# A two-layer decoder step with experts: gather without gaps, shared down products later, gather batches of four passes

## Chip, cores and metric

The kernel runs on 1 core of a Trainium2 chip. The metric is the device time of one execution in microseconds, median of the runs.

## What is computed

One inference step of a two-layer decoder for 320 tokens (256 of a prompt, 64 of 8 sampled sequences), model width 1024: layer 0 mixes with sliding-window attention, layer 1 with gated linear attention. Each is followed by the mixture of experts that this study is about:

```python
def moe(h, router_w, router_b, wg, wu, wd, swg, swu, swd):
...
    scores = jax.nn.sigmoid((x @ router_w).astype(jnp.float32))
    sel = scores + router_b.astype(jnp.float32)
...
    _, eidx = lax.top_k(jnp.where(emask, sel, -jnp.inf), TOP_K)
    w = jnp.take_along_axis(scores, eidx, axis=1)
    w = w / jnp.sum(w, axis=-1, keepdims=True) * ROUTED_SCALE
    routed = routed_experts(x, eidx, w.astype(x.dtype), wg, wu, wd)
    shared = (jax.nn.silu(x @ swg) * (x @ swu)) @ swd
    return (routed + shared).reshape(B, S, D)
```

`emask` leaves the best 4 of 8 groups of experts, so each token goes to 8 of 64 experts. An expert has gate and up weights of 1024 x 256 each (2 MB together in float32) and down weights of 256 x 1024 (1 MB). All 64 experts of both layers are read once: 3 MB x 64 x 2.

## The kernel before

Everything is in one `decoder_step`. `moe(l)` first routes: it counts the tokens of each expert, ranks the experts by their counts (ranks 0 and 1 are fixed experts whose weights are loaded ahead), and writes the ranking to `order`. Then 28 passes follow, with 128 slots each. A pass holds two or three experts by rank: `pass_plan` gives (96, 32), (64, 64) or, at the places `LIGHT_AT`, (64, 32, 32) slots. `posS` holds for each token and expert the slot of the token in the expert's list, and `excess` whether any expert has more tokens than its slots; then `rest` goes through all 64 experts once more.

What one pass does on TensorE (PE), in `moe`, from L2026 on:

- *gate product* (L2044): the pass's tokens from the buffer `xg`, in groups of 32 or 64 columns, times the gate and up weights of its experts, 8 steps over the model width, into bank `W0`.
- *fills* (L1946): part of the gather for the next batch of passes. The gather is a product of the token rows (`htok`, `htok2`, high and low parts, five matmuls) with a selection matrix `sel` (a one where slot and token meet). A batch is 2 or 4 passes (`BATCHES`), so 256 or 512 columns; a batch needs 8 fills, one per 128 rows of the model width (batch 0: 4 fills with two rows blocks each). ScalarE (ACT) and VectorE (DVE) copy the fills in turns from banks `W1` and `W2` to `xg` (L2110, L2169), in which each fill overwrites tokens already used.
- *turning* (L2070): `hh`, which DVE made from `W0` (silu by ACT at L2127, product and weight by DVE at L2209), is transposed; ACT copies it to `hTs`. In a batch's last pass the slot weights of the next batch are made too (`slot_weights`, L1956), from the selection in bfloat16, `selb`, which DVE makes in `dense`.
- *combine* (L1974, L1976): the last pass's result (`yhi`, `ylo`) is added to the tokens' sums, by a product with `gt`, 12 matmuls.
- *down product* (L2094), into `W1` and `W2`. ACT and DVE then take them to `yhi` and `ylo`.
- in passes 1 and 2 the shared expert's down products, `shared_down` (L2022), which add to the same sums.

DVE makes the selections of the batch after the next (`select`, L2149 and L2154, then `dense`, L2163) at the end of a batch's last pass.

The weights are moved by one queue, issued by SyncE (SP) in `expert_stream`. Gate and up weights go to `gu_ring`, 6 places of 2 MB; down weights to `dn_ring`, 5 places of 1 MB. Ahead of the wait for `order` come the down and gate/up weights of ranks 0 and 1 and the shared expert's down weights (L1605, 1 MB, in the fifth place). Behind it `load_up` (L1614) and `load_down` (L1622) alternate in the order of the passes. A place is free again when the pass that used it has made its gate product (`gu_full`) or its down product (`y_full`), the fifth place when `shd_used` tells that the shared products are made. SyncE issues strictly in order, so a load that waits for a place holds all behind it. `DN_EARLY` = 4 down loads need no free place.

## Time and profile before

| | us |
|---|---|
| median of 3 runs | 1434.81 (1434.44 to 1436.46) |
| profiled execution | 1434.92 |
| its span, first to last instruction | 1433.1 |
| PE busy | 1395.9 (97%) |
| DVE busy | 437.7 (31%) |
| ACT busy | 317.1 (22%) |
| queue of SyncE | 489.96 MB, 82.1% of the span of 16 engines |

The span is 1.8 us shorter than the time of the same execution. The passes of layer 0 take from 247.5 to some 706 us, those of layer 1 from 954.5 to 1412. PE's busy time is no rate: a matmul that is in the array counts as busy. A window's GB/s tells how full the transfers' side is.

### The profile page before, as it was taken

Reading aid. Unit: us, or ns where it says so; the run is one execution under the profiler, and the core shown is the slowest. Engines: PE = TensorE matmul, PEld = TensorE weight load, DVE = VectorE, ACT = ScalarE, POOL = GpSimd, SP = SyncE. Lnnn points to the kernel's source line nnn. Section 1 sums busy time; section 2 is a strip of 40 time slices with the busy share of each in tenths; the row PEclk is TensorE's granted clock in tenths of the full one; section 3 lists DMA queues with packets and bytes.
Section 4 is the critical chain, followed back from the end, with each engine's and each line's share of the span. In section 5 each row is a group of like instructions: output and inputs, shape, how many; then the busy total and the mean of one; then the engine's idle time right before and its main releaser. Section 6 shows DMA issues by size and latency. Waiting matters only on the chain.

```text
span 1433.1 us, 20787 instructions
## 1 busy us (share of the span) xinstructions
PE 1395.9 (97%) x8288; PEld 706.4 (49%) x8288; DVE 437.7 (31%) x1161; ACT 317.1 (22%) x746; POOL 48.1 (3%) x86
## 2 busy tenths in 40 slices
PE   7999999999999999999999999999999999999997
PEld 3345657444445444444465456564444444444443
DVE  1146535312221222122345243442121312122214
ACT  2134323111111111111345113411111111111113
POOL 0100302000000000000100010010000000000000
PEclk9999999999999999999999999999999999999998
DMA  9999528999999999999972245389999999999993
GB/s 393 389 381 427 214 103 311 392 390 427 421 423 426 421 425 425 424 426 424 422 320 118 118 162 219 112 336 380 425 424 423 426 423 421 425 424 426 425 424 126
DMA packets 48002, 509.52 MB, mean 356 GB/s; under 512 B 5808, under 2 KB 6208, under 8 KB 8320
## 3 DMA queue, kind: packets, MB, share of 16 engines
q1 hardware_dynamic: 44144, 489.96, 82.1%
q0 software_dynamic: 3760, 18.20, 3.4%
q8 instruction: 68, 1.11, 0.3%
q14 instruction: 30, 0.25, 0.0%
HBM read 499.10 MB, written 11.01 MB: 356 GB/s over the span
## 4 chain that ended last, share of the span: by engine, by line
PE 88%; DMA 4%; DVE 3%; ACT 3%; issue 1%; SPq 0%; DVEq 0%; ACTq 0%
PE bank L2044 26%; PE banks L2094 13%; PE banks L1946 10%; PE banks L442 5%; PE ybank L1974 3%; PE banks L1119 3%; PE banks L1974 3%; PE bank L1976 3%; DMA s_gu_ring<-in_moe_up_dram 3%; PE bank L504 2%; PE ybank L1738 1%; PE banks L1738 1%; DMA s_gu_ring<-in_ada_w_dram 1%; PE banks L697 1%; PE banks L1124 1%; PE banks L671 1%
## 5 line engine op out<-in xcount | busy, mean ns | idle before, releaser
L2044 PE MATMUL bank<-s_gu_ring,s_hbuf 128*32 128x512 f32 (+1 forms) x2688 | 395.2, 593 | 1.4 <-DVE s_hbuf L2169 0.9
L2044 PEld LDWEIGHTS bank<-s_gu_ring,s_hbuf 128*32 128x32 f32 (+1 forms) x2688 | 121.9, 119 | 265.9 <-issue 265.9
L2094 PE MATMUL banks<-s_dn_ring,s_hTs 128*32 128x512 f32 (+1 forms) x1344 | 204.2, 596 | 0.0
L2214 DVE TENSOR_TENSOR s_ylo<-banks,s_yhi 128x512 fp32r<-128x512 f32 x112 | 77.5, 692 | 320.2 <-ACT s_yhi L2136 320.2
L1946 PE MATMUL banks<-s_sel,s_htok 128*128 128x512 f32 (+1 forms) x640 | 144.8, 374 | 0.5 <-issue 0.5
L1946 PEld LDWEIGHTS banks<-s_sel,s_htok 128*128 128x128 f32 x640 | 106.2, 188 | 60.7 <-issue 44.3
L2136 ACT CAST s_yhi<-banks 128x512 fp32r<-128x512 f32 x112 | 65.7, 586 | 296.5 <-PE banks L2094 296.5
L2209 DVE SCALAR_TENSOR_TENSOR s_hh<-s_sg,s_wsl,bank 128x256 f32<-128x256 f32 x56 | 26.9, 480 | 288.1 <-ACT s_sg L2127 288.1
L2094 PEld LDWEIGHTS banks<-s_dn_ring,s_hTs 128*32 128x32 f32 (+1 forms) x1344 | 55.9, 118 | 118.0 <-issue 117.3
L2127 ACT ACTIVATE s_sg<-bank 128x256 f32<-128x256 f32 x56 | 21.6, 385 | 364.8 <-PE bank L2044 364.8
L2169 DVE COPY s_hbuf<-banks 128x512 f32<-128x512 f32 (+1 forms) x60 | 39.4, 656 | 96.0 <-PE banks L1946 96.0
L1119 PE MATMUL banks<-s_gu_ring,s_hbuf 128*128 128x512 f32 x128 | 55.9, 593 | 0.5 <-DVE s_rs L1439 0.5
L2110 ACT COPY s_hbuf<-banks 128x512 f32<-128x512 f32 (+1 forms) x60 | 33.5, 559 | 57.9 <-PE banks L1946 57.9
L1974 PE MATMUL ybank<-s_yhi,s_gt 128*128 128x512 f32 x108 | 38.7, 439 | 0.0
L1119 PEld LDWEIGHTS banks<-s_gu_ring,s_hbuf 128*128 128x128 f32 x128 | 24.2, 191 | 29.1 <-issue 28.2
L504 PE MATMUL bank<-s_gu_ring,s_condT 128*32 128x512 f32 x288 | 34.9, 598 | 1.2 <-DMA s_gu_ring<-in_ada_w_dram 1.2
L2131 ACT COPY s_hTs<-bank 128x256 f32<-128x256 f32 x56 | 20.9, 373 | 64.0 <-PE bank L2070 43.1
L442 PE MATMUL banks<-s_hbuf,s_gu_ring 128*128 128x320 f32 x128 | 34.9, 433 | 0.0
L442 PE MATMUL banks<-s_qk,s_gu_ring 128*128 128x320 f32 x128 | 34.9, 433 | 0.0
L1974 PE MATMUL ybank<-s_ylo,s_gt 128*128 128x512 f32 x108 | 33.9, 395 | 0.0
L1974 PE MATMUL banks<-s_yhi,s_gt 128*128 128x512 f32 x108 | 33.9, 395 | 0.0
L1974 PE MATMUL banks<-s_ylo,s_gt 128*128 128x512 f32 x108 | 33.6, 392 | 0.0
(463 smaller groups left out, 1452.5 us busy)
## 6 DMA issues: line engine op xcount, KB each, us to landing
s_gu_ring<-in_moe_up_dram SPq DMA_DIRECT2D x128, 2048.0 KB, 15.2
s_dn_ring<-in_moe_wd_dram SPq DMA_DIRECT2D x128, 1024.0 KB, 12.8
s_gu_ring<-in_ada_w_dram SPq DMA_DIRECT2D x24, 2048.0 KB, 13.0
s_gu_ring<-in_win_dram SPq DMA_DIRECT2D x6, 2048.0 KB, 12.8
s_gu_ring<-in_wqkv_dram SPq DMA_DIRECT2D x6, 1024.0 KB, 19.4
s_gu_ring<-in_wo_dram SPq DMA_DIRECT2D x2, 2048.0 KB, 18.8
s_gu_ring<-in_shared_up_dram SPq DMA_DIRECT2D x2, 2048.0 KB, 9.8
s_gu_ring<-in_gwo_dram SPq DMA_DIRECT2D x2, 2048.0 KB, 10.8
```

The source lines that it names most:

```text
L442: last = pe.matmul(b[:, 0:T], item(slot)[:, k, (m % 4) * P:(m % 4 + 1) * P], src[:, k, :], start=(k == 0), stop=(k == KC - 1))
L504: last = pe.matmul(ada_bank(n)[32 * j:32 * j + 32, :], condT[:, k, lo:lo + 32], item(s)[:, k, :], start=(x == 0 and kk == 0), stop=(ends_g ...
L1119: last = pe.matmul(b[:, :], hT[:, k, t0:t0 + P], w[:, k, :], start=(k == 0), stop=(k == KC - 1))
L1946: last = pe.matmul(b[:, width * x:width * x + width], w[:, m * P:(m + 1) * P], sel[:, s, 0:width], start=(n == 0), stop=(n == 4))
L1974: last = pe.matmul(acc[(t, half)], g[:, t * P:(t + 1) * P], y[:, half, :], start=(p == 0 and y is yhi), stop=False)
L1976: last = pe.matmul(bank[6][:, :], g[:, 320 - 64 * half:448 - 64 * half], y[:, half, :], start=(p == 0 and y is yhi and half == 0), stop=False)
L2044: last = pe.matmul(W0[o:o + n, :], tokens_of(p, k)[:, o:o + n], w[:, k, :, :], start=(k == 0), stop=(k == KC - 1))
L2094: last = pe.matmul((W1, W2)[half][o:o + n, :], hTs[:, f, o:o + n], dn_ring[:, DN_PLACE[dn_of[(l, r)][0]], w0:w0 + 512], start=(f == 0), st ...
L2110: act.copy(fill_target(q, f), fill_source(q, f)).then_inc(S["fill_act"], 1)
L2136: act.copy(yhi[:, half, :], (W1, W2)[half]).then_inc(S["y_high"], 1)
L2169: dve.tensor_copy(fill_target(q, f), fill_source(q, f)).then_inc(S["fill_dve"], 1)
L2214: dve.tensor_tensor(ylo[:, half, :], (W1, W2)[half], yhi[:, half, :].bitcast(F32), ALU.subtract).then_inc(S["y_low"], 1)
```

## The change

Four things are changed, all in the expert part of both layers.

1. *Packed gather.* `ROOMS` gives a room to each rank of each layer, at most its slots, and `PITCH` a width to each batch: 112 columns a pass in batch 0, 104 in the others. `sel` has only the rooms, side by side, so fills are 448 or 416 columns wide. The gate product still has groups of 32 or 64 columns; it reads them from the packed place (`back_by`). The bfloat16 selection keeps 128 slots a pass: `spread` (in place of `dense`) zeroes it and copies each expert's columns to their slots. The gap columns of `xg` are zeroed once per layer. `excess` is now against the rooms.
2. *Batches.* Seven of four passes. Batch 0 has 8 fills of four passes ahead of pass 0, and passes 0 and 1 carry two fills each in place of four. Passes 24 to 27 carry none.
3. *Shared expert.* Its down weights are loaded within the stream, in a place of `dn_ring` that becomes free behind pass 16 in layer 0, and its down products are in passes 18 and 19. `DN_EARLY` is 5.
4. The pairs of experts in a pass are put together in another order; the numbers of experts and slots of each pass stay. `sg` and `hTs` now lie in the free space of `router`, and `selb` is one tile.

```diff
-NGU, NDN, DN_EARLY = 6, 5, 4
+NGU, NDN, DN_EARLY = 6, 5, 5
...
+PITCH = (112, 104, 104, 104, 104, 104, 104)
...
+def gathered(l, experts):
+
+    out, at = [], 0
+    for r, cap, o in places(experts):
+        out.append((r, ROOMS[l][r], o, at))
+        at += ROOMS[l][r]
+    return out
...
-BATCHES = (2, 4, 4, 4, 4, 4, 4, 2)
+SHD_PASS = 18
+BATCHES = (4,) * 7
...
-NFILL = 4 + 8 * (NB - 1)
+NFILL = 8 * NB
...
-            freed = [None] * (NDN - 1) + [2]
+            freed = [None] * NDN
+            shd_at = sum(len(experts) for experts in PASSES[l][:SHD_PASS + 1])
...
+                if i == shd_at:
+                    d = i % NDN
+                    down_in[d].n += 16
+                    shd_of.append((d, down_in[d].n, last_dn[d]))
+                    last_dn[d], freed[d] = (S["shd_used"], l + 1), SHD_PASS + 1
+                d = (i + (i >= shd_at)) % NDN
+                used = None if i < NDN else last_dn[d]
...
-                sp.dma_start(dn_ring[:, DN_PLACE[NDN - 1], :], a["shared_down"][l]).then_inc(down_in[NDN - 1].h, 16)
...
+                    if shd_of[l][2] == (S["y_full"], 2 * (l * NP + p + 1)):
+                        d, _, used = shd_of[l]
+                        sp.wait_ge(*used)
+                        sp.dma_start(dn_ring[:, DN_PLACE[d], :], a["shared_down"][l]).then_inc(down_in[d].h, 16)
...
-                        width = P * BATCHES[q]
...
+                        width = PITCH[q] * BATCHES[q]
+                        for n, (w, s) in enumerate(shown):
+                            last = pe.matmul(b[:, 0:width], w[:, f * P:(f + 1) * P], sel[:, s, 0:width], start=(n == 0), stop=(n == 4))
...
-                    for f in range(4):
+                    for f in range(8):
...
-                        fill_some(turns[:3])
-                        if p == 2:
+                        fill_some(turns)
+                        if p == SHD_PASS + 1:
...
-                        fill_some(turns[3:])
...
-                        if p == 1:
-                            pe.wait_ge(down_in[NDN - 1].h, shd_n)
+                        if p == SHD_PASS:
+                            pe.wait_ge(down_in[shd_d].h, shd_n)
...
+                    def spread(q):
+
+                        step(dve.memset(selb[:, :, 0:P * BATCHES[q]], 0.0))
+                        w = PITCH[q]
+                        for h in range(BATCHES[q]):
+                            for r, n, o, at in gathered(l, PASSES[l][BATCH_START[q] + h]):
+                                last = dve.tensor_copy(selb[:, :, h * P + o:h * P + o + n], sel[:, :, h * w + at:h * w + at + n].bitcast(F32))
                         return last
...
+                    dve.wait_ge(S["fill_full"], filled(0, 1))
+                    dve.memset(hbuf[:, :].rearrange("p (x s) -> p x s", s=P)[:, :, PITCH[0]:P], 0.0)
+                    for f in range(1, 8, 2):
+                        fill_out(0, f)
```

How the order of instructions moves. On SyncE, ahead of the first load of layer 0 that needs the order (`s_order` is the ranking, `ISA` reads it into a register), before:

```order
L1598 DMA s_dn_ring<-in_moe_wd_dram 128x2048 x2
L1602 DMA s_gu_ring<-in_moe_up_dram 128x4096 x2
L1605 DMA s_dn_ring<-in_shared_down_dram 128x2048
L1610 TENSOR_LOAD s_order
L1610 ISA x2
```

And in the changed kernel the shared expert's load, which stands behind the three gate/up loads that pass 16 of layer 0 lets go:

```order
L1633 ISA x2
L1637 ISA
L1637 DMA s_gu_ring<-in_moe_up_dram 128x4096
L1660 DMA s_dn_ring<-in_shared_down_dram 128x2048
L1641 TENSOR_LOAD s_order
```

The 1 MB load has moved from ahead of the stream of expert loads into it, where down loads stand behind it.

On PE, from the last fill ahead of pass 0 of layer 0 through pass 0 (gate product, fills, turning, down product), before:

```order
L1946 MATMUL banks<-s_sel,s_htok_0 128x256
...
L1956 MATMUL bank<-s_wpartS,s_selb 128x18
L2044 MATMUL bank<-s_gu_ring,s_hbuf 64x512 x16
L1946 MATMUL banks<-s_sel,s_htok 128x512 x4
L1946 MATMUL banks<-s_sel,s_htok_0 128x512
...
L2070 MATMUL bank<-s_cst,s_hh 128x128 x2
...
L2094 MATMUL banks<-s_dn_ring,s_hTs 64x512 x8
```

And now:

```order
L1964 MATMUL banks<-s_sel,s_htok_0 128x448
L1973 MATMUL bank<-s_wpartS,s_selb 128x12 x3
L1973 MATMUL bank<-s_wpartS,s_selb 128x18 x6
...
L2061 MATMUL bank<-s_gu_ring,s_hbuf 64x512 x16
L1964 MATMUL banks<-s_sel,s_htok 128x416 x4
...
L2087 MATMUL bank<-s_cst,s_hh 128x128 x2
L2110 MATMUL banks<-s_dn_ring,s_router 64x512 x8
```

Each fill is a row of four and a row of one; pass 0 had four such pairs of 512 columns, three ahead of the turning and one behind, and has two of 416.

On DVE, ahead of the copies that empty the first fills of layer 0, before:

```order
L2149 TENSOR_TENSOR s_sel<-s_cst,s_posS 128x3x128
...
L2178 TENSOR_TENSOR s_wpartS<-s_hh,s_wpartS 128x3x64
L2163 CAST s_router<-s_sel 128x256 x2
L2163 CAST s_selb<-s_sel 64x256
L2182 TENSOR_TENSOR s_ovh<-s_ovh,ybank 128x320
L2169 COPY s_hbuf<-banks 128x2x256 x2
```

And now:

```order
L2163 TENSOR_TENSOR s_sel<-s_cst,s_posS 128x3x60
...
L2189 TENSOR_TENSOR s_wpartS<-s_hh,s_wpartS 128x3x64
L2170 MEMSET s_selb 128x768
L2174 CAST s_selb<-s_sel 128x3x60
L2174 CAST s_selb<-s_sel 128x3x52
...
L2193 TENSOR_TENSOR s_ovh<-s_ovh,ybank 128x320
L2196 MEMSET s_hbuf 128x32x16
L2180 COPY s_hbuf<-banks 128x4x112 x4
```

Four selections have become ten, three casts a zeroing and ten casts (of which two are shown), and the gap columns are zeroed ahead of the copies.

## Rows read from the trace of the kernel before

**Rows 1.** The page, sections 1 and 2 (DMA: busy tenths in 40 slices).

```profile
PE 1395.9 (97%) x8288; PEld 706.4 (49%) x8288; DVE 437.7 (31%) x1161; ACT 317.1 (22%) x746; POOL 48.1 (3%) x86
...
DMA  9999528999999999999972245389999999999993
```

**Rows 2.** Windows: us, busy per engine (instructions), PEclk, DMA share, GB/s.

```profile
237.00:310.00 73.00, 72.31 (x442) 36.99 (x445) 24.17 (x69) 10.73 (x23) 0.00 (x0) 1.00 0.95 394
310.00:692.00 382.00, 381.65 (x2396) 178.19 (x2392) 87.98 (x214) 59.58 (x125) 0.00 (x0) 1.00 1.01 424
943.00:1010.00 67.00, 66.30 (x394) 35.36 (x394) 22.21 (x62) 9.70 (x21) 0.00 (x0) 1.00 0.95 389
1010.00:1398.00 388.00, 388.00 (x2254) 181.92 (x2253) 89.23 (x216) 60.27 (x126) 0.00 (x0) 1.00 1.01 424
```

**Rows 3.** Chain of waits at the end of layer 0 (start us, us, what).

```profile
670.33 21.34 DMA s_gu_ring<-in_moe_up_dram
```

**Rows 4.** Timeline of PE, passes 26 and 27 of layer 0.

```profile
687.81 3.64 PE L2094 MATMUL banks<-s_dn_ring,s_hTs 128*32 128x512 f32 x32
691.80 7.07 PE L2044 MATMUL bank<-s_gu_ring,s_hbuf 128*32 128x512 f32 x64 [0.35 <-DMA s_gu_ring<-in_moe_up_dram]
```

**Rows 5.** Three gate/up loads of layer 0, by tile and window.

```profile
L1614 SPq DMA_DIRECT2D s_gu_ring<-in_moe_up_dram x1: 338/338/338, 241.6 to 241.6; - x1
...
DMA to landing us min/median/max: 15.2/15.2/15.2
...
L1614 SPq DMA_DIRECT2D s_gu_ring<-in_moe_up_dram x1: 347/347/347, 254.8 to 254.8; - x1
...
DMA to landing us min/median/max: 7.7/7.7/7.7
...
L1614 SPq DMA_DIRECT2D s_gu_ring<-in_moe_up_dram x1: 338/338/338, 270.5 to 270.5; - x1
...
DMA to landing us min/median/max: 9.3/9.3/9.3
```

**Rows 6.** Chain of waits, layer 0, first fills to pass 4.

```profile
241.58 5.04 PE banks L1946 x40
...
270.25 3.63 PE banks L1946 x15
...
282.76 3.63 PE ybank L2022 x8
286.39 7.00 PE bank L2044 x64
...
295.91 3.43 PE banks L2022 x8
299.34 1.87 PE bank L2022 x8
...
307.98 6.87 PE bank L2044 x64
...
323.91 6.42 PE bank L2044 x57
```

**Rows 7.** Timeline of DVE ahead of pass 0, layer 0.

```profile
241.83 0.49 DVE L2182 TENSOR_TENSOR s_ovh<-s_ovh,ybank 128x320 f32<-128x320 f32 x1 [1.17 <-ACT s_ovh L1814]
...
248.32 2.31 DVE L2154 TENSOR_TENSOR s_sel<-s_cst,s_posS 128x192 fp32r<-128x192 f32 x9
```

**Rows 8.** Groups of instructions by form, DVE, the casts of L2163.

```profile
L2163 DVE CAST s_router<-s_sel 128x512 bf16<-128x512 f32 x24 | 9.2, 423 | 0.4
...
L2163 DVE CAST s_router<-s_sel 128x256 bf16<-128x256 f32 x8 | 2.0, 288 | 0.1
```

**Rows 9.** Line L360 on PE (ns min/median/max, first to last start).

```profile
L360 PE MATMUL banks<-s_sq,s_cst x32: 432/445/457, 194.5 to 720.7; 128*32 128x320 f32 x32
...
L360 PE MATMUL ybank<-s_sq,s_cst x16: 433/741/742, 8.2 to 12.6; 128*32 128x320 f32 x16
```

**Rows 10.** Windows, the end of the span.

```profile
1430.00:1433.00 3.00, 0.00 (x0) 0.00 (x0) 0.00 (x0) 0.00 (x0) 0.00 (x0) 0.50 0.74 243
```

More of the change, by code:

```diff
@@ L1927, in fills_in @@
                         return []
-                    return range(4 * j, 4 * j + 4) if q == 0 else range(2 * j, 2 * j + 2)
+                    return range(2 * j, 2 * j + 2)
                 def last_of(p):
@@ L2199, in _ @@
                     step(select(1))
-                    dense(1).then_inc(S["sel_full"], 1)
+                    spread(1).then_inc(S["sel_full"], 1)
                     dve.wait_ge(S["wall_full"], l * NB + 1)
```

108 lines of the change are left out of this document (41 added, 67 removed), and 6 rows, old and new, of the table ROOMS.

## The prediction

> **What bounds the kernel now.** I read the page first: TensorE is busy for 97% of the span, and in the long stretches of expert work the DMA line stands at 9 as well [rows 1]. Two resources are full at once, so the share of busy time does not say which of them sets the end. The windows are read next. From 310 to 692 us the transfers run at 424 GB/s without a dip, and so do those of layer 1 from 1010 to 1398; in the stretches ahead of these (237 to 310, 943 to 1010) the means are only 394 and 389 GB/s [rows 2]. The lost time there is 73 x (1 - 394/424) = 5.2 us and 67 x (1 - 389/424) = 5.5 us. Third, the chain at the end of layer 0: the last pass starts when the gate/up weights of its last expert land; the chain goes back through this transfer for 21.34 us [rows 3]. That transfer was issued 21 us before it landed, so it did not wait for a free place, it waited for the transfers in front of it. The matmuls were nearly as late: pass 26's down products end at 687.81 + 3.64 = 691.45, and the wait from there is 0.35 us [rows 4]. So both resources reach the last pass together, and the transfers are the later one. From here on, time comes off only if **the stream of weight transfers ends earlier**.
>
> What ends the stream: it begins when the sorted order is known, moves fixed bytes at 424 GB/s, and loses time only where the queue runs empty because a place in the ring is not free yet. The sixth gate/up load is issued at 241.6 and lands 15.2 us later, at 256.8. The next needs the place of pass 0's expert, is issued at 254.8, and lands 7.7 us after it, at 262.5 [rows 5]. One such load takes 2,097,152 B / 424 GB/s = 4.9 us when the queue is full; so a load that finds the queue empty starts 2.8 us after its issue, and 262.5 - 256.8 - 4.9 = 0.8 us is lost here. The two other losses of layer 0 follow the long passes 1 and 2: pass 2 starts at 286.39 and pass 3 at 307.98 [rows 6], 21.6 us apart, where a pass of the steady loop takes 15.9 us (307.98 to 323.91). In passes 1 and 2 PE also runs the shared expert's down products, in pass 1 double fills too.
>
> **The change, part by part.**
>
> *Shared down weights.* Their 1 MB is loaded today before the order is known, when the queue has nothing else. Now it sits inside the stream: 1,048,576 B / 424 GB/s = **+2.5 us per layer**. The fifth early down load moves 1 MB ahead of the first empty queue; it adds no bytes, but prefetch now lasts until 256.8 + 2.5 = 259.3.
>
> *Shared down products.* They cost 3.63 + 3.43 + 1.87 = 8.9 us on PE [rows 6]. They leave passes 1 and 2 and come back in 18 and 19: nothing for PE's sum, but the places of passes 1 and 2 come free earlier.
>
> *Packed gather.* 15 fill matmuls of 512 columns take 3.63 us, 0.242 each, and 40 of 256 columns 5.04 us, 0.126 each [rows 6]: 0.45 ns a column. At 416 columns a fill matmul costs 0.199, at 448 0.213. A steady pass has 10: -0.43 us. PE per layer: passes 0 and 1 lose 20 matmuls of 512 (-4.8) and 2 x 0.43; passes 2 to 21 20 x 0.43 = -8.6; passes 22 and 23 widen from 256 to 416 (+1.5); passes 24 and 25 have none (20 x 0.126 = -2.5). Sum -15.3 us. All of it lies beside the transfers, so I cost it at nothing; its cover is the stream, and what PE gains turns into waits for weights.
>
> *The first batch.* Pass 0 cannot start before all 8 fills of four passes: 40 x 0.213 = 8.5 us in place of 5.0, +3.5; six more small weight matmuls, +0.5. VectorE now makes ten selections (1,344 elements) in place of four (768), zeroes the spread copy, copies ten pieces, then zeroes the gap columns of the token buffer before it may empty the second bank. Selections cost 1.05 ns an element and 0.08 us each, by nine with 1,536 elements in 2.31 us [rows 7]: +1.0 us. The zeroing isn't in the trace: 768 words at between nothing and that rate, up to 0.8; the copies, 1.4 to 2.2 by the rates of a cast (288 ns for 256 elements, 423 for 512: 0.53 ns an element [rows 8]) and of a selection. The chain today ends with the product at 241.83 + 0.49 = 242.3 [rows 7]; the new one at about 243.5 to 244.8, then gap columns 0.2 to 0.6 and the copy out 0.6. The fourth fill should start at 241.6 + 3 x 1.07 = 244.8, and would then start at up to 246.1. So pass 0 starts **4.1 us later** (no delay by VectorE) **to 5.4**; I take 5.0, nearer to the high end since every piece of that chain is a small instruction.
>
> The Trainium skill says in "VectorE: DVE Perf Modes" (What auto-detection actually checks) that a copy with one source may double its rate when source and destination are in SBUF and their outermost dimensions agree, which these copies meet; the 0.53 ns a cast pays today agrees. By the page alone the copies take the lower 1.4 us and pass 0 starts some 0.5 us earlier.
>
> *Effect on the empty queue.* Issue of the first load that needs a freed place: 254.8 + 5.0 = 259.8, start 262.6, queue empty since 259.3: **3.3 us** lost, 2.4 to 3.7 by the bounds. Pass 0 has two fills where it had four and shrinks to about 13.5 us (7.0 gate product, 2.0 fills, 0.9 turning, 3.6 down product), so pass 1 starts at 266.0 and frees its three places at 273.1, while the down loads before run until 277.4. Today the load issued at 270.5, just behind two down loads, lands 9.3 us after its issue, 1.6 us more than the lone one [rows 5], so a narrow margin does not help fully. With 4 us I take a loss of 0.3, and 0 to 1 as bounds. Later passes are 15.5 us and issue well ahead. So 3.6 us per layer replace 5.2 and 5.5.
>
> **Sum.** Layer 0: -5.2 + 3.6 + 2.5 = +0.9; layer 1: -5.5 + 3.6 + 2.5 = +0.6. Together +1.5 us on the profiled execution's 1434.92, and the median of the runs is 0.1 lower: **1436.3 us**. With all bounds: 2 x (2.4 + 2.5) - 10.7 = -0.9, and 2 x (4.7 + 2.5) - 10.7 = +3.7. PE is ready for the last pass 15.3 - 5.0 = some 10 us before its weights, less what it waits earlier (the down weights of passes 2 and 18, which stand behind gate/up loads or the shared MB in the queue). SyncE's added issue costs nothing, since transfers there wait some 10 us in the queue.
>
> **Rivals.** *The clock falls in the new waits (slower).* PE now idles for some 4 us ahead of pass 27 of both layers. No idle stretch of that length lies between the passes today. At the start, where PE comes out of idleness, the 128x320 matmuls from 8.2 to 12.6 us show a median of 741 ns against 445 later [rows 9], so some 4 us ran slow; and in the span's last 3 us, with PE done, the granted clock is 0.50, the 1.2 GHz level [rows 10]. If pass 27 restarts so, half of that is lost, 2 us per layer and 4 in all: 1440.3. It decides from a wait of that order on; for it speaks that waits gather at the end of the layer, against it that passes 2, 16 and 18 may take most of the 10 us, where lost clock only shortens the later wait. The Trainium skill, "TensorE: Matmul & The Clock Gate" (HAM oscillation), has this rule: waiting for a DMA between bursts of matmuls sends the clock to 1.2 GHz, and the next burst starts cold. By it I give this 15%.
>
> *The early losses vanish (faster).* If pass 0 starts no more than 1.7 us later and nothing is lost behind pass 1, the whole 10.7 us is saved and 5.0 paid: 1429.1. Half of it gives 1432. The four-pass first batch speaks against it; for it speaks that pass 2 alone starts 5 us earlier than today even so. 17% for over 0.2%.
>
> *VectorE becomes late at each batch.* After a batch's last pass it selects (2.0 us), zeroes (to 0.8) and spreads (1.4 to 2.0), starting 1.8 us into a gate product of 7.0 us: done at 6.0 to 6.9, in time. If it overran by 2.5 us, six times a layer, 15 us would exceed PE's 10 us of slack: +5 per layer, 1446. 9%.
>
> *The rooms are too small.* Then the loop over 64 experts runs: 64 x 3 MB at 424 GB/s is 475 us. Working through the routing of the reference's inputs gives no expert above its room: 1%.
>
> **How the numbers follow.** No change beyond 0.2% (2.9 us, about what a measurement can tell) is the likeliest, 58% for this case with 1433.9 to 1438.6 as its own range, of which 5 in 58 lie over the bound. Faster 17; same 53; slower 5 + 15 + 9 + 1 = 30. The range leaves one in ten on each side: 1431.5 to 1440.5.
>
> **What would show it.** Right: 424 GB/s from about 280 us on in layer 0, one dip near 260, none near 293; pass 0 about 5 us later, pass 3 about 10 us earlier (near 297); waits of PE for weight transfers of some 8 to 10 us per layer, where now there is 0.4; last pass still released by its gate/up transfer, within 1.5 us of 691.8. Wrong: a last pass that starts right behind pass 26, a dip at 293 that stays, or a granted clock below 1.00 behind the waits.

## The result and the profile after

| | before | after |
|---|---|---|
| median, us | 1435.16 (12 runs, 1434.44 to 1436.67) | 1438.35 (12 runs, 1437.21 to 1441.09) |
| ratio, with its 95% interval | | 1.002 [1.0012, 1.0028] |
| profiled execution, us | 1434.92 | 1437.59 |
| its span, us | 1433.1 | 1435.8 |
| PE busy, us | 1395.9 | 1379.5 |

The change costs 3.2 us, 0.22%, just over the 0.2% that can be told from nothing. TensorE's busy time shrank by 16.4 us and the end came later. The chain that ended last, section 4 of the page of the kernel before:

```profile
PE 88%; DMA 4%; DVE 3%; ACT 3%; issue 1%; SPq 0%; DVEq 0%; ACTq 0%
```

And the page of the kernel after, its sections 1, 2, 4 and 5 (to be held against [rows 1]):

```profile
PE 1379.5 (96%) x8208; PEld 705.5 (49%) x8208; DVE 445.2 (31%) x1281; ACT 312.2 (22%) x740; POOL 48.0 (3%) x86
...
DMA  9999526999999999999972245279999999999992
...
PE 77%; DMA 14%; DVE 4%; ACT 3%; issue 1%; SPq 1%; DVEq 0%; ACTq 0%
...
L2061 PE MATMUL bank<-s_gu_ring,s_hbuf 128*32 128x512 f32 (+1 forms) x2688 | 397.1, 596 | 8.1 <-DMA s_gu_ring<-in_moe_up_dram 7.1
...
L2110 PE MATMUL banks<-s_dn_ring,s_router 128*32 128x512 f32 (+1 forms) x1344 | 207.6, 602 | 12.3 <-DMA s_dn_ring<-in_moe_wd_dram 11.4
```

The last numbers of the two lower rows are TensorE's waits ahead of the gate products (L2061) and the down products (L2110): 18.5 us for weight transfers, over both layers. In the chain the transfers' share rose from 4 to 14%. The span grew by 2.7 us while the busy time fell by 16.4, so TensorE stood idle for 19.1 us more, nearly all of it in these waits. The windows of the kernel after (us, busy per engine, granted clock, DMA share, GB/s), beside [rows 2]:

```profile
237.00:310.00 73.00, 69.35 (x460) 37.61 (x461) 25.13 (x81) 11.77 (x26) 0.00 (x0) 1.00 0.97 408
310.00:692.00 382.00, 375.07 (x2328) 176.63 (x2326) 91.82 (x264) 56.32 (x119) 0.00 (x0) 1.00 1.01 425
553.30:556.50 3.20, 3.20 (x10) 1.20 (x8) 0.00 (x0) 0.12 (x1) 0.00 (x0) 0.50 1.01 430
692.00:699.00 7.00, 6.76 (x48) 2.37 (x52) 0.00 (x0) 0.00 (x0) 0.00 (x0) 0.76 1.04 433
940.00:1010.00 70.00, 66.05 (x421) 36.45 (x423) 24.94 (x83) 11.80 (x25) 3.99 (x2) 1.00 0.96 403
1010.00:1400.00 390.00, 384.51 (x2214) 183.38 (x2206) 92.89 (x266) 57.72 (x123) 0.00 (x0) 1.00 1.01 425
```

Two things are to be seen. The early dip is shallower than before, but still there: 73 x (1 - 408/425) = 2.9 us in layer 0 and 70 x (1 - 403/425) = 3.6 us in layer 1, where it was 5.2 and 5.5. And the granted clock is no longer 1.00 all through the layers: it is 0.50, the 1.2 GHz level, in a window of pass 18 of layer 0 (and in one of pass 18 of layer 1, from 1263.2 us), and on the mean 0.76 in the seven microseconds around the start of pass 27 of layer 0. The timeline of PE in the kernel after, at four places (start us, us, line, then in brackets the wait ahead of it). They are the start of the count, pass 18 of layer 0, and pass 27 of both layers:

```profile
224.38 0.20 PE L1782 MATMUL bank<-s_mb,s_upper_b 128*128 128x64 bf16 x1 [0.61 <-ACT s_htok L1831]
...
552.92 5.35 PE L2110 MATMUL banks<-s_dn_ring,s_router 128*64 128x512 f32 x16 [3.40 <-DMA s_dn_ring<-in_moe_wd_dram]
...
692.24 8.77 PE L2061 MATMUL bank<-s_gu_ring,s_hbuf 128*32 128x512 f32 x64 [3.32 <-DMA s_gu_ring<-in_moe_up_dram]
...
1401.32 7.07 PE L2061 MATMUL bank<-s_gu_ring,s_hbuf 128*32 128x512 f32 x64 [3.21 <-DMA s_gu_ring<-in_moe_up_dram]
```

The third and fourth rows are the same product, pass 27's, in layer 0 and layer 1. Behind a wait of 3.32 us it takes 8.77 us, behind one of 3.21 us 7.07, the value that it had before [rows 4]. The difference, 1.70 us, is the fall of the clock: it stands at 0.50 from 693.2 to 696.6 us, and half of these 3.4 us is lost. Pass 18's product shows the same: 5.35 us, where it takes 3.65 in run noload1, whose clock didn't fall there.

The first row gives a mark: L1782 is the first product of the count of the tokens, with which the expert part of a layer begins. With it and the start of pass 27, an execution falls into pieces that can be compared between kernels. A is from the count to pass 27 of layer 0, B from there to the count of layer 1, C from there to pass 27 of layer 1, D from there to the end. All from the timelines of PE, in us:

| kernel | A | B | C | D | span |
|---|---|---|---|---|---|
| before | 467.5 | 239.5 | 467.4 | 34.4 | 1433.1 |
| after | 467.9 | 241.2 | 467.9 | 34.5 | 1435.8 |

In these two kernels pass 27 starts when its weights land, so A and C show the transfers' side; B and D show what the clock costs behind that. Of the 2.7 us that the span grew by, 0.35 are in A, 0.53 in C, and **1.7 in B**. B is the 1.70 us of pass 27's gate product.

The first load that waits for a freed place, in the kernel after (queue and landing, as in [rows 5]):

```profile
L1637 SPq DMA_DIRECT2D s_gu_ring<-in_moe_up_dram x1: 341/341/341, 259.4 to 259.4; - x1
...
DMA to landing us min/median/max: 7.9/7.9/7.9
```

The transfer ahead of it landed at 259.7, it landed at 267.3; a full queue takes 4.9 us for it, so 2.7 us are lost. The same reading behind pass 1 (issued at 272.9, landed 5.8 us behind the one ahead of it) gives 0.9. The third loss, behind pass 2, is not seen any more: that pass's freed places are filled behind a full queue (a load issued at 275.1 lands 17.7 us later).

### The profile page after: what moved, and what is told of

Its sections match the earlier page's. It is cut to its first block, busy times and chain, and to the rows that moved or that the text cites. A ratio compares the mean times of both kernels' runs of the same rounds, so it can differ in the third digit from the quotient of the medians.

```text
span 1435.8 us, 20741 instructions
## 1 busy us (share of the span) xinstructions
PE 1379.5 (96%) x8208; PEld 705.5 (49%) x8208; DVE 445.2 (31%) x1281; ACT 312.2 (22%) x740; POOL 48.0 (3%) x86
## 4 chain that ended last, share of the span: by engine, by line
PE 77%; DMA 14%; DVE 4%; ACT 3%; issue 1%; SPq 1%; DVEq 0%; ACTq 0%
PE bank L2061 22%; PE banks L2110 12%; DMA s_gu_ring<-in_moe_up_dram 7%; PE banks L1964 6%; DMA s_dn_ring<-in_moe_wd_dram 6%; PE banks L459 5%; PE banks L1136 3%; PE ybank L1991 3%; PE banks L1991 3%; PE bank L1993 3%; PE bank L521 2%; PE banks L1764 1%; DMA s_gu_ring<-in_ada_w_dram 1%; PE banks L714 1%; PE banks L1141 1%
## 5 line engine op out<-in xcount | busy, mean ns | idle before, releaser
L2061 PE MATMUL bank<-s_gu_ring,s_hbuf 128*32 128x512 f32 (+1 forms) x2688 | 397.1, 596 | 8.1 <-DMA s_gu_ring<-in_moe_up_dram 7.1
L2061 PEld LDWEIGHTS bank<-s_gu_ring,s_hbuf 128*32 128x32 f32 (+1 forms) x2688 | 124.1, 119 | 272.3 <-issue 272.3
L2110 PE MATMUL banks<-s_dn_ring,s_router 128*32 128x512 f32 (+1 forms) x1344 | 207.6, 602 | 12.3 <-DMA s_dn_ring<-in_moe_wd_dram 11.4
L1964 PEld LDWEIGHTS banks<-s_sel,s_htok 128*128 128x128 f32 x560 | 100.5, 188 | 44.7 <-issue 42.5
L2110 PEld LDWEIGHTS banks<-s_dn_ring,s_router 128*32 128x32 f32 (+1 forms) x1344 | 57.7, 119 | 131.7 <-issue 130.4
L1964 PE MATMUL banks<-s_sel,s_htok 128*128 128x416 f32 (+1 forms) x560 | 120.9, 363 | 1.2 <-DVE s_hbuf L2180 0.7
L2222 DVE SCALAR_TENSOR_TENSOR s_hh<-s_router,s_wsl,bank 128x256 f32<-128x256 f32 x56 | 26.9, 480 | 287.7 <-ACT s_router L2143 287.7
L2143 ACT ACTIVATE s_router<-bank 128x256 f32<-128x256 f32 x56 | 21.5, 385 | 373.4 <-PE bank L2061 373.4
L2180 DVE COPY s_hbuf<-banks 128x416 f32<-128x416 f32 (+1 forms) x56 | 33.3, 594 | 64.8 <-PE banks L1964 64.8
L2126 ACT COPY s_hbuf<-banks 128x416 f32<-128x416 f32 (+1 forms) x56 | 28.6, 510 | 47.8 <-PE banks L1964 47.8
L2147 ACT COPY s_router<-bank 128x256 f32<-128x256 f32 x56 | 20.9, 374 | 66.4 <-PE bank L2087 35.5
## 6 DMA issues: line engine op xcount, KB each, us to landing
s_gu_ring<-in_moe_up_dram SPq DMA_DIRECT2D x128, 2048.0 KB, 21.5
s_gu_ring<-in_wo_dram SPq DMA_DIRECT2D x2, 2048.0 KB, 19.1
```

The source lines that it names most:

```text
L1964: last = pe.matmul(b[:, 0:width], w[:, f * P:(f + 1) * P], sel[:, s, 0:width], start=(n == 0), stop=(n == 4))
L2061: last = pe.matmul(W0[o:o + n, :], tokens_of(p, k)[:, o - back_by[r]:o - back_by[r] + n], w[:, k, :, :], start=(k == 0), stop=(k == KC - 1))
L2110: last = pe.matmul((W1, W2)[half][o:o + n, :], hTs[:, f, o:o + n], dn_ring[:, DN_PLACE[dn_of[(l, r)][0]], w0:w0 + 512], start=(f == 0), st ...
L2126: act.copy(fill_target(q, f), fill_source(q, f)).then_inc(S["fill_act"], 1)
L2180: dve.tensor_copy(fill_target(q, f), fill_source(q, f)).then_inc(S["fill_dve"], 1)
```

## The experiments

Theory: the end of A and C is set by the stream of transfers, with three terms (the time that the queue runs empty at the start, the shared expert's megabyte in the stream, the moment at which pass 0 frees its place); B and D pay for falls of the clock behind waits ahead of the last passes. Rivals: TensorE or VectorE, late since pass 0, carries that to the end; or the clock is without effect. The eleven runs take the change apart along its parts ("packed" takes in the new order of the pairs, part 4, which no run separates from the packing). In run noload only layer 0 can be read; the other ten are in the table, with the pieces of their profiled executions. Four kernels (late, b24pre, pre, preawake) have 1.5 to 1.7 us in B from a fall of the clock between the layers, near 877 us, in a stage that no run changed; the last section comes back to it.

| kernel | packed | shared late | batches | A | B | C | D | span |
|---|---|---|---|---|---|---|---|---|
| before | no | no | of 2, 4 | 467.5 | 239.5 | 467.4 | 34.4 | 1433.1 |
| late | no | yes | of 2, 4 | 467.0 | 241.2 | 467.1 | 34.4 | 1433.8 |
| b24pre | yes | no | of 2, 4 | 467.9 | 242.6 | 466.9 | 36.1 | 1438.2 |
| b24 | yes | yes | of 2, 4 | 464.9 | 241.2 | 464.2 | 37.3 | 1432.2 |
| pre | yes | no | of 4 | 467.7 | 243.7 | 468.1 | 36.0 | 1439.7 |
| after | yes | yes | of 4 | 467.9 | 241.2 | 467.9 | 34.5 | 1435.8 |
| awake | as after | | | 467.9 | 239.5 | 468.0 | 34.4 | 1434.6 |
| preawake | as pre | | | 467.8 | 242.7 | 468.4 | 34.4 | 1437.5 |
| b24awake | as b24 | | | 466.2 | 239.5 | 464.2 | 34.4 | 1428.7 |
| best | as b24 | | | 464.2 | 239.5 | 464.1 | 34.4 | 1426.5 |
| b24wait | as b24 | | | 469.7 | 240.8 | 469.9 | 37.1 | 1441.7 |
| noload1 | as after | | | 467.8 | 240.9 | 465.2 | 36.1 | 1434.3 |

### awake: no bare wait ahead of pass 27

```diff
                         if l * NP + p:
                             pe.wait_ge(S["hT_full"], l * NP + p)
+                        if p == NP - 1:
+                            keep_awake(pe, W0, 14)
```

`keep_awake` is the kernel's own helper (L437): products of 128 columns into a bank that the gate product overwrites. Each of them stands in the trace as two matmuls.

> Theory (the stream of the experts' transfers sets the end, and the fall of the clock behind the 3.3 us wait ahead of pass 27 is paid on top): 14 products without a use in that wait keep the granted clock at 1.0, pass 27 and the combination behind it run at full speed, and 1.6 us come off in layer 0 and nothing in layer 1, whose wait of 3.18 us was followed by no fall in the profiled execution; 1436.7 us beside 1435.2 of the kernel before, ratio 1.001. If the fall comes in both layers in most executions, 3.2 us come off: 1435.1, ratio 1.000. Rival (the clock matters nowhere, since TensorE has time to spare): 1438.3, ratio 1.002.

Measured: 1435.68 us (11 runs) beside 1435.56, ratio 1.0002 [0.9993, 1.0011]; the change's own interval, [1.0012, 1.0028], lies wholly above it. The change's excess over before is gone: 0.1 us is left of 3.2. Timeline of PE ahead of pass 27 of layer 1, and the window of pass 27 in layer 0:

```profile
1396.86 3.39 PE L440 MATMUL bank<-s_cst 128*128 128x128 f32 x28
1400.18 7.07 PE L2063 MATMUL bank<-s_gu_ring,s_hbuf 128*32 128x512 f32 x64
```

```profile
692.00:699.00 7.00, 7.00 (x67) 2.88 (x69) 0.00 (x0) 0.00 (x0) 0.00 (x0) 1.00 1.04 428
```

The clock stays at 1.00 where it was 0.76. A and C are those of after within 0.13 us: the added products take nothing from the transfers' side; B is back at 239.5. The medians differ by 2.7 us (3.1 when each is held against the kernel before in its own session), where one fall costs 1.7, so some executions of the changed kernel seem to have more than one; the profiled one had one that costs. All twelve of them (from 1437.21 us) lie at least 1.9 us above the fastest of awake (1435.34). The fall of pass 18 (at 554.2 and 1260.8 in this trace) is still there and costs nothing at the end, since TensorE waits again before pass 27. The rival "the clock matters nowhere" is out.

### noload and noload1: the price of the megabyte

```diff
 # noload, in both layers; noload1 the same for l == 1 only
-                    down_in[d].n += 16
...
-                        sp.dma_start(dn_ring[:, DN_PLACE[d], :], a["shared_down"][l]).then_inc(down_in[d].h, 16)
```

> Leaves out the shared expert's load of 1 MB; its products are done with whatever lies in that place. Theory (stream): the last gate and up weights land 2.5 us sooner in each layer, 5.0 in all: 1433.3 us, ratio 0.9987; with the shorter wait ahead of pass 27 (0.8 us instead of 3.3) the clock doesn't fall there either, and 1.6 more come off: 1431.7, ratio 0.9976. Rival (TensorE or VectorE, late by the 5 us of the late start, carries that to the end): 1438, ratio 1.002, and no idle time ahead of pass 27 changes.

Measured: 4275.49 us. The time as a whole says nothing: with layer 0's result changed, layer 1 routes otherwise, and the loop over all 64 experts, which is entered when a room is too small, runs from 1440 to 4243 us. Only layer 0, which is not touched by that, can be read: from the count (224.03) to pass 27 (689.45) it takes 465.4 us where the change takes 467.9. That is 2.45 us for 1 MB. To have the same within a whole execution, the load was left out in layer 1 only:

> The change without the shared expert's load of layer 1 (whose products are done with whatever lies in that place); layer 0 is left whole, so that the routing of layer 1 is that of the reference. Theory (stream, a megabyte at 424 GB/s): the last weights of layer 1 land 2.5 us sooner, 466.0 us behind the start of its stage in place of 468.5, and the wait ahead of pass 27 shrinks to 0.7 us: 1435.1 to 1435.8 us, ratio 1.000. Rival (TensorE ends near the stream): the last 1 us or so of it is not had, 1437, ratio 1.001.

Measured: C = 465.2 in place of 467.9, 2.7 us less, and A unchanged at 467.8. That is the stream's price of the megabyte, as the theory had it. But the time is 1438.4 us, ratio 1.0013 [1.0003, 1.0022], not 1.000. The timeline of PE at pass 27 of layer 1 says why:

```profile
1398.22 8.73 PE L2062 MATMUL bank<-s_gu_ring,s_hbuf 128*32 128x512 f32 x64 [4.87 <-DMA s_gu_ring<-in_moe_up_dram]
```

My expectation of a shorter wait was wrong. Here is the down product of pass 18 of layer 1, in the change first, then in noload1:

```profile
1262.07 5.35 PE L2110 MATMUL banks<-s_dn_ring,s_router 128*64 128x512 f32 x16 [3.44 <-DMA s_dn_ring<-in_moe_wd_dram]
1258.98 3.65 PE L2111 MATMUL banks<-s_dn_ring,s_router 128*64 128x512 f32 x16 [0.98 <-DMA s_dn_ring<-in_moe_wd_dram]
```

Without the load TensorE waits 2.46 us less there, and the clock doesn't fall, which saves another 1.70. So it comes to pass 27 some 4.2 us sooner, the weights only 2.7; it waits 4.87 us, not 3.21, the clock falls, and the product takes 8.73 us, not 7.07. A wait taken from one pass turned up in the last, where it costs. Layer 0 of this run, whose edit is that of the change, shows what a fall in pass 18 does for the last wait: in this execution the clock fell in pass 2 (behind a wait of 1.94 us) and not in pass 18, and the wait ahead of pass 27 is 4.96 us, where the change's, behind a fall in pass 18, is 3.32.

### late, b24pre, b24: which part of the change does what

`late` is the kernel before with the shared part alone (the lines of the diff above on `DN_EARLY`, `SHD_PASS`, `shd_at` and `shd_of`, and nothing else), `b24pre` the kernel before with the packed gather alone (and the new order of the pairs), `b24` both with the old batches. Against the changed kernel b24 is (in all kernels of this form the last expert's selection in a pass reaches to the pass's width, so that no column of `sel` is left unwritten):

```diff
-PITCH = (112, 104, 104, 104, 104, 104, 104)
+PITCH = (112, 112, 104, 104, 104, 104, 104, 104)
...
-BATCHES = (4,) * 7
+BATCHES = (2, 4, 4, 4, 4, 4, 4, 2)
...
-NFILL = 8 * NB
+NFILL = 4 + 8 * (NB - 1)
...
-                        fill_some(turns)
+                        fill_some(turns[:3])
...
+                        fill_some(turns[3:])
```

> The kernel before with the late shared load and products alone: batches and unpacked gather as before. Theory (two limits near each other): the stream has a place more full at its start and loses 3.8 us less there, against 2.5 us for the shared megabyte in it; but TensorE's work, which ended 0.35 us ahead of the last weights before, becomes the limit, and the late products still stand in it: the same as before or up to 1 us slower, 1435.2 to 1436.5, ratio 1.000 to 1.001. Rival (the stream alone bounds): 1.3 us less per layer, 1432.6, ratio 0.998. Rival (the megabyte costs its 2.5 us in full): 5 more, 1440, ratio 1.0035.

> The packed gather alone: shared load and products, and the batches, as in the kernel before. Theory (TensorE and the stream both end near 691 us of layer 0 in the kernel before, and with the packing the stream alone is left): the last weights land where the kernel before has them or up to 1.5 us sooner per layer, since nothing in the stream is changed but places that come free sooner; with waits of 3 to 4 us ahead of passes 26 and 27 the clock falls behind them, as in the run pre, which costs up to 2 us per layer: 1433 to 1438 us, likeliest 1436, ratio 1.000. Rival (TensorE's work bounds the kernel before, so the 15 us of it that the packing saves in each layer come off in part): 1425, ratio 0.993.

> The batches of the kernel before (2, 4, 4, 4, 4, 4, 4, 2) with the packed gather and the late shared products kept. Theory (stream): pass 0 starts some 4.7 us sooner, near 247.5, the first load that waits for a place is issued near 255 and no longer finds the queue empty (2.7 us of loss gone, at most 1 left behind pass 1): the last weights land 1.7 to 2.7 us sooner in each layer, 1433 to 1435 us, ratio 0.9985 to 1.0; the wait ahead of pass 27 gets no shorter, so the clock may fall as before. Rival (the batches are at no fault: the queue runs empty for another reason, as the time from a place coming free to the landing): same as the change, 1438, ratio 1.002.

Measured: late 1434.11 us, ratio 0.9988 [0.9979, 0.9998]; b24pre 1440.02 us, ratio 1.0027 [1.0016, 1.0038]; b24 1431.71 us, ratio 0.9967 [0.9955, 0.9979].

*late.* Its window of the early passes and its timeline at the end of layer 0:

```profile
237.00:310.00 73.00, 72.30 (x479) 38.80 (x478) 25.21 (x71) 11.96 (x26) 0.00 (x0) 1.00 1.01 426
```

```profile
687.69 3.64 PE L2104 MATMUL banks<-s_dn_ring,s_hTs 128*32 128x512 f32 x32
691.14 2.33 PE L2054 MATMUL bank<-s_gu_ring,s_hbuf 128*32 128x512 f32 x20
```

```profile
PE 91%; DVE 3%; ACT 3%; DMA 1%; issue 1%; SPq 0%; DVEq 0%; ACTq 0%
```

426 GB/s from the start, so the early loss of 5.2 us [rows 2] is gone in full. What is left of it in A is 0.5 us: pass 27 starts right behind pass 26 with no wait, and the chain (third fence) holds 1% of transfers, beside 4% before. TensorE is the limit, and it ends only 0.5 us ahead of where the transfers did. B is 1.7 us longer than before, though pass 27's product takes 7.05 us: this execution, the slowest of the ten, has the fall between the layers. I had expected no gain; 1.1 us came in the median. The rival by which the transfers alone bound the kernel before is out, and so is the one with the full 2.5 us per layer.

*b24pre.* Windows of the early passes and of pass 26 of layer 0, then the timeline of passes 26 and 27:

```profile
237.00:310.00 73.00, 72.06 (x454) 37.39 (x456) 26.49 (x88) 10.46 (x23) 0.00 (x0) 1.00 0.97 398
672.10:678.90 6.80, 6.00 (x32) 1.67 (x36) 0.00 (x0) 0.00 (x0) 0.00 (x0) 0.50 1.02 424
```

```profile
672.90 10.02 PE L2064 MATMUL bank<-s_gu_ring,s_hbuf 128*32 128x512 f32 x64 [2.90 <-DMA s_gu_ring<-in_moe_up_dram]
...
692.60 7.85 PE L2064 MATMUL bank<-s_gu_ring,s_hbuf 128*32 128x512 f32 x56 [2.91 <-DMA s_gu_ring<-in_moe_up_dram]
```

The early dip stays (398 GB/s beside 394), A and C move by +0.4 and -0.5, and TensorE, with less to do, waits ahead of passes 26 and 27, and the clock falls there. (The second row is cut by the end of its view: the whole product of 64 matmuls takes 8.71 us.) The packing alone makes the kernel 4.8 us slower, 2 us beyond the slow end of what I expected: it gives the stream nothing (I had reckoned with up to 1.5 us per layer), and pays 3.1 us in B, of which 1.6 are pass 27's product and 1.5 the fall between the layers, and 1.7 in D. The rival (it saves TensorE's time at the end) is out.

*b24.* Both together: window of the early passes and of the end of layer 1, pass 27 of layer 1 in the timeline, and the first load that waits for a place:

```profile
237.00:310.00 73.00, 72.07 (x492) 39.46 (x494) 27.56 (x90) 11.74 (x26) 0.00 (x0) 1.00 1.01 426
1393.90:1400.70 6.80, 5.84 (x28) 1.59 (x32) 0.00 (x0) 0.00 (x0) 0.00 (x0) 0.50 0.86 357
```

```profile
1394.86 9.96 PE L2071 MATMUL bank<-s_gu_ring,s_hbuf 128*32 128x512 f32 x64 [4.75 <-DMA s_gu_ring<-in_moe_up_dram]
```

```profile
L1637 SPq DMA_DIRECT2D s_gu_ring<-in_moe_up_dram x1: 341/341/341, 255.1 to 255.1; - x1
...
DMA to landing us min/median/max: 9.8/9.8/9.8
```

Issued 4.3 us sooner than in the changed kernel, that load lands 9.8 us later, behind a full queue: nothing is lost, and A and C are 2.6 and 3.1 us below those before. By the terms: 5.2 and 5.5 us of early losses gone, 2.5 of the megabyte added, -2.7 and -3.0. That is more than I expected of the run, since no loss at all is left behind pass 1 either. The late shared part frees the stream, but TensorE is then the limit and hides it; the packing frees TensorE, but the stream is then the limit and hides it; **only both together move the end**. And the seven batches then cost 3.0 and 3.7 us of it again (467.9 and 467.9 against 464.9 and 464.2). In D this kernel pays 2.9 us, for a stretch of 6.8 us at 0.50 that begins within the wait of 4.75: the product takes 9.96 us and not 7.07.

### pre and preawake: the shared part undone

`pre` is the change with the shared load ahead of the stream and its products in passes 1 and 2, as before:

```diff
-NGU, NDN, DN_EARLY = 6, 5, 5
+NGU, NDN, DN_EARLY = 6, 5, 4
...
-SHD_PASS = 18
+SHD_PASS = 1
...
                 stored.wait(sp)
+                sp.dma_start(dn_ring[:, DN_PLACE[NDN - 1], :], a["shared_down"][l]).then_inc(down_in[NDN - 1].h, 16)
                 sp.wait_ge(S["order_full"], l + 1)
```

`preawake` is the same with 12 products ahead of passes 26 and 27:

```diff
+                        if p >= NP - 2:
+                            keep_awake(pe, W0, 12)
```

> The shared load ahead of the stream and its products in passes 1 and 2, as in the kernel before; packed gather and seven batches kept. Theory (stream): the shared megabyte leaves the stream (2.5 us less) but one place less is full at the start, so the queue runs empty 2.5 us longer before the first freed place: the same within 0.5 us per layer, 1438, ratio 1.002. Rival (the late shared products at pass 18 and 19, with their load in the stream, are the whole of the change's loss): 2.5 less per layer, 1433.3, ratio 0.9987.

> The run pre (shared part undone, packed gather and seven batches kept) with 12 products without a use (2.9 us) ahead of the gate products of passes 26 and 27. Theory (pre's 2.7 us over the change are all clock: in its profile pass 27 of layer 0 starts 468.35 us behind the start of the stage as in the change with 468.47, and the clock is at half speed for 28 us of the layers and the stages between them): the falls at passes 26 and 27 go, and with them some 5 us: 1436, ratio 1.0005. Rival (undoing the shared part is slow by its stream or by TensorE's early passes): 1441, ratio 1.0035, with or without the products.

Measured: pre 1441.01 us, ratio 1.0035 [1.0021, 1.0048]; preawake 1439.13 us, ratio 1.0022 [1.0012, 1.0032]. The pieces A and C of pre stand within 0.2 us of after's, as the theory has it (megabyte against empty queue), but not its time: 2.7 us more than the change in the median, 3.9 in the profiled executions, all of it in B and D. Of that 1.7 are the fall between the layers; the rest are longer products of pass 27 (9.55 us in layer 0, 8.65 in layer 1). Passes 26 and 27 of layer 0, pre first, then preawake:

```profile
672.29 8.77 PE L2054 MATMUL bank<-s_gu_ring,s_hbuf 128*32 128x512 f32 x64 [3.73 <-DMA s_gu_ring<-in_moe_up_dram]
691.95 8.27 PE L2054 MATMUL bank<-s_gu_ring,s_hbuf 128*32 128x512 f32 x52 [4.11 <-DMA s_gu_ring<-in_moe_up_dram]
```

```profile
672.34 7.08 PE L2056 MATMUL bank<-s_gu_ring,s_hbuf 128*32 128x512 f32 x64 [0.83 <-DMA s_gu_ring<-in_moe_up_dram]
686.13 2.94 PE L440 MATMUL bank<-s_cst 128*128 128x128 f32 x24
692.00 8.34 PE L2056 MATMUL bank<-s_gu_ring,s_hbuf 128*32 128x512 f32 x60 [2.92 <-DMA s_gu_ring<-in_moe_up_dram]
```

The products covered the wait of pass 26; TensorE was then 1.7 us sooner at pass 27, where 2.94 us of them left 2.92 us bare, and the clock fell there (the rows of pass 27 are cut by the end of the view; whole, they take 9.55 and 8.77 us). In layer 1 a bare wait of 2.95 us was left and the clock did not fall: 7.07 us. So 1.9 us of some 5 came back, less than I expected: in the profiled execution 1.7 of what is left are pass 27's product and 1.5 the fall between the layers, which these products couldn't touch. That more of them would bring the rest was not tried here. That undoing the shared part would win 2.5 us per layer (the rival of pre) is out.

### b24wait: the late start alone

```diff
+                        if p == 0:
+                            keep_awake(pe, W0, 20)
```

> b24 with 20 products without a use ahead of the gate product of pass 0, 4.8 us: the late start of the change without its batches. Theory (the late start of pass 0 is what the seven batches cost, through places that come free 4.7 us later): the queue runs empty for some 3 to 3.5 us again before the first freed place, from the start of the stage to pass 27 468 to 468.5 us as in the change in place of 465.5 and 464.9, 1437 to 1438.4 us, ratio 1.0015 to 1.0022. Rival (it is something else in the batches: the fills of eight chunks in four passes, the work of VectorE): 1432, ratio 0.997, the same as b24.

Measured: 1443.55 us, ratio 1.005 [1.0034, 1.0065]. Pass 0 starts at 252.13, as in the change (252.18), and the early window is at 402 GB/s, where b24 has 426:

```profile
237.00:310.00 73.00, 72.13 (x505) 40.23 (x504) 26.75 (x89) 10.79 (x25) 0.00 (x0) 1.00 0.97 402
```

The late start alone brings the dip back, so the work of the larger batches on VectorE and in the fills isn't needed to explain it. The size was off: A and C rise by 4.8 and 5.7 us, not by 3 to 3.5. In the change passes 0 and 1 have two fills each and take 13.45 + 15.54 = 29.0 us, here 15.08 + 18.89 = 34.0, so every place behind pass 0 comes free still later. By these rows the seven batches cost 4.8 and 5.7 us by their late start, and the change stands 1.8 and 2.0 us below this run; that it's the shorter passes which give that back is argued from their lengths, not tried alone.

### b24awake and best: does it add up

```diff
+                        if p == NP - 1:
+                            keep_awake(pe, W0, (10, 16)[l])
```

> The packed gather, the late shared products and the batches of the kernel before (as in b24), with products without a use in the wait ahead of pass 27: 10 in layer 0, 16 in layer 1 (14 of them took 3.39 us in the run awake). Theory (the stream sets when the weights land, the clock what the last pass costs after that): b24's profiled execution fell to half speed for 3.5 us at pass 27 of layer 0 and for 6.8 us at that of layer 1, some 1.7 and 3 us; both go, 1427 to 1429 us, ratio 0.9945. If products of that kind do nothing where the wait is 4.7 us long: 1431.7, ratio 0.997.

Measured: 1430.53 us, ratio 0.9961 [0.9948, 0.9973], 1.5 us beyond the slow end of what I expected. B and D are at 239.5 and 34.4, the values without a fall; but A has grown by 1.3 us over b24. In this execution the clock fell at pass 18 for 6.8 us (549.9 to 556.7) and not for 3.4, and the products ahead of pass 27 ended only then: with them TensorE came later than the weights. The next kernel covers pass 18 as well, and has 14 products ahead of pass 27 in both layers:

```diff
+                        if p == SHD_PASS:
+                            keep_awake(pe, W0, 8)
                         for r in ranks:
                             d, n, _ = dn_of[(l, r)]
                             pe.wait_ge(down_in[d].h, n)
```

> b24 (packed gather, late shared products, batches of the kernel before) with products without a use in two waits of each layer: 8 (1.9 us) ahead of the down product of pass 18, 14 (3.4 us) ahead of the gate product of pass 27. Theory: the stream gives the 465.5 and 464.9 us from the start of the stage to pass 27 that b24 had; no fall of the clock between them or behind, so 238.9 us between the layers and 34.4 at the end, as in the run awake: a span of 1427.4 us, a time of 1429.2, ratio 0.9955. b24awake, with the wait in pass 18 left bare, had a fall of 6.8 us there and was 1.2 us slower in layer 0; that goes. Rival (products in pass 18 only push TensorE back and it ends late at pass 27): 1430.5 or more, ratio 0.996 or above.

Measured: 1428.56 us (5 runs, 1428.20 to 1430.32) beside 1436.53, ratio 0.9952 [0.9938, 0.9965]. Windows of the early passes, of pass 18 and of pass 27 of layer 1, then the timeline ahead of the latter:

```profile
237.00:310.00 73.00, 72.07 (x490) 39.33 (x493) 27.43 (x90) 11.60 (x26) 0.00 (x0) 1.00 1.01 427
...
549.00:560.00 11.00, 9.34 (x35) 3.48 (x36) 1.96 (x5) 1.17 (x2) 0.00 (x0) 1.00 0.99 420
1390.00:1403.00 13.00, 11.59 (x93) 5.61 (x95) 0.48 (x1) 0.76 (x2) 0.00 (x0) 1.00 0.61 252
```

```profile
1387.75 2.96 PE L440 MATMUL bank<-s_cst 128*128 128x128 f32 x25
...
1392.12 7.07 PE L2073 MATMUL bank<-s_gu_ring,s_hbuf 128*32 128x512 f32 x64 [1.42 <-DMA s_gu_ring<-in_moe_up_dram]
```

The granted clock is 1.00 from the count of layer 0 to the end of pass 27 of layer 1, and none of the kernels has a shorter piece. (The x25 of the timeline should be 28; some matmuls are missing from a trace.) This version beats both the kernel before, by 0.5%, and the changed one. It is the change without its second part (the batches stay those of before), plus 22 products per layer whose results nobody reads.

## Why the prediction was right, and where not

Forecast: 1436.3 us, within 0.2% of before, range 1431.5 to 1440.5. Measured: 1438.35, in the range, but 0.22% above before and so a hair past "no change"; the likeliest case's own range (to 1438.6) just holds it. The number came near for a sum that is not the forecast's: the stream's part was smaller than forecast (0.9 us in the trace for 1.5), and the clock, which the sum had at nothing, put some 3 us on top (by run awake). Point by point:

- *The stream ends each layer.* Right for the changed kernel: pass 27 is released by its gate/up transfer in both layers, 0.44 us later than before in layer 0 (692.24 beside 691.80), within the 1.5 us named. Not the whole of it for the kernel before: run late shows TensorE as a second limit, 0.5 and 0.3 us behind the first, so 0.8 us in both layers was all that the stream could have given alone. The prediction saw the 0.35 us wait [rows 4] and drew from it only that the transfers are later; "time comes off only if the stream ends earlier" held for less than 1 us, and past that TensorE's work counts too.
- *Late start.* 5.0 us forecast, 4.7 measured (252.18 beside 247.51). It lies in the bounds of 4.1 to 5.4. VectorE's chain went as reckoned: the zeroing took 0.70 us (up to 0.8 forecast), the ten copies 1.63 (1.4 to 2.2), its product ended at 244.0 (243.5 to 244.8), and TensorE waited 0.35 us for it.
- *First loss.* 3.3 forecast, 2.7 measured; behind pass 1 0.3 forecast, 0.9 measured. Together 3.6, as forecast; that the sum came out is luck, since both terms were off by 0.6 in opposite directions. The windows give less for layer 0, 2.9 us. The loss behind pass 2 is gone, pass 3 starts at 298.83 (forecast near 297, later by the wait of 2.1 us for down weights in pass 2).
- *The megabyte.* 2.5 us forecast, 2.45 and 2.7 measured.
- *Sum of the stream.* +0.9 and +0.6 forecast, +0.35 and +0.53 measured in A and C.
- *TensorE's 15.3 us per layer at no gain.* The amount was right: with the longer start, 2 x (15.3 - 4.0) = 22.6 us of busy time should go; 16.4 went, and the three falls of the clock in this execution lengthen the busy time by 3 x 1.7 = 5.1 us, so 21.5 by that. Waits of 18.5 us in both layers, forecast 16 to 20. Run b24pre shows that the packing alone brings no time. Beside the late shared part it does, 2.4 us (1434.11 in late, 1431.71 in b24), so "at nothing" holds only as long as the transfers are the limit.
- *VectorE, and the rooms.* Neither rival came. The price of the latter was far off: the loop over 64 experts took 2803 us in run noload (1440 to 4243), some 44 us per expert, not 475 us in all by its bytes.
- **The step that failed** is "its cover is the stream, and what PE gains turns into waits for weights", costed at nothing. The waits cost clock. A granted clock below 1.00 behind the waits was on the prediction's own list of signs of being wrong, and it is there. The rival had the mechanism, the place (ahead of pass 27) and nearly the price (2 us per layer; 1.7 in the rows), but I gave it 15%, and put its decision at a wait of "that order". Run awake, which takes only this away, leaves 0.1 us over the kernel before where the change has 3.2. The argument against it, that earlier passes would take most of the 10 us, was wrong in its conclusion: in layer 0 they took 2.1 and 3.4 us, and 3.3 were left. Right in it was that a fall in pass 18 only shortens the later wait: without one that wait is 4.96 us (noload1, layer 0). One row that the rival rested on is weaker than it was taken for: the matmuls from 8.2 to 12.6 us take 741 ns [rows 9], but the windows of the kernel before show a granted clock of 1.00 there, so their slowness isn't shown to be the clock's.

Without the clock the forecast would have stood: the rise in the stream is 0.9 us in the trace, the medians of awake and before differ by 0.1. What stays open: how many falls a given execution has. The profile shows one that costs in the changed kernel; the medians (2.7 to 3.1 us between after and awake) say 1.6 to 1.8. The mean granted clock of each execution points the same way: six of the twelve have 0.995, as the profiled one, and take 1437.2 to 1438.4 us, the other six have 0.991 to 0.993 and take 1438.3 to 1441.1. It counts also falls that cost nothing, so it settles no number.

## What to carry to other kernels

When two resources end together, an edit that relieves one is worth little and may lose: here the shared part alone gave 0.1%, the packing alone cost 0.3%, both together gave 0.3%, and with the clock held 0.5%. Before counting relief of TensorE as free, look where its waits will gather: ahead of the last pass they cost mostly 1.4 to 2.9 us each where the clock fell, and products without a use in them win that back if they end before the data come. An earlier wait that is taken away, or covered, can come back there. And where a ring feeds a stream, the first freed place decides: a start that is some 4.6 us late (b24wait) cost 4.8 and 5.7 us, more than the megabyte's 2.5 to 2.7.

## What the runs showed of the hardware

- The granted clock fell to 0.50 in or behind bare waits of 2.9 to 5.0 us, and in the expert parts also behind 2.42 us (b24, pass 27 of layer 0, product 8.77 us) and 1.94 us (noload1, pass 2 of layer 0, down product 5.34 us and not 3.64). It didn't fall behind a wait of 3.21 us (after, pass 27 of layer 1), nor behind 2.42 us (after, pass 2 of layer 1, with 3.64 us for the down product). Behind 2.95 us ahead of pass 27 of layer 1 it fell in pre (8.65 us) and not in preawake (7.07). Waits of the same length do both, so a price for them is a chance, not a rule.
- The stretches at 0.50 in the expert parts were 3.4 or 6.8 us long. The gate product of pass 27 takes 7.07 us without one, 8.4 to 8.8 with one of 3.4 and 9.6 to 10.0 with one of 6.8 us. Where a part of the stretch lies in the wait, the product pays for less than half of it. The Trainium skill says in "TensorE: Matmul & The Clock Gate" (HAM oscillation) that matmul bursts between waits for a DMA start cold; these traces agree, with the reservation that it isn't so each time.
- Run late has a half-speed stretch from 874.4 to 877.8 us, between the layers, and its piece B is 1.7 us longer for it. It occurs in pre, preawake and b24pre as well, in a stage that no experiment touched. Its cause was not looked for. Executions of the kernel before may have it too: most of them lie near 1435.1 us with a mean clock of 0.998 or near 1436.5 with 0.996; no trace here shows it.
- A load issued into an empty queue lands 7.7 to 7.9 us after its issue in three kernels, of which 4.9 are its bytes at the rate of a full queue; the 2.8 to 3.0 us that are left are an estimate of what passes ahead of them.
